# A two-block transformer kernel: pointwise work of the mixers done behind the tiles of the input projection, and the modulation sums of block two moved

## The reference, cut to what matters

```python
mod = cond @ ada_w[l] + ada_b[l]          # six vectors: sh1, sc1, g1, sh2, sc2, g2
h = _rms_norm(x, norm1_g[l]) * (1.0 + sc1) + sh1
pa, pb, pc, pd = _split(h @ w_in[l], GROUP_COLS)
# a, recurrent mixer
p = p + (p_prev - p) * mu                 # shift by one token, all of group a
w_log = -softplus(-(w0 + tanh(wd) @ w_up)) - 0.5
a = sigmoid(a0 + ad @ a_up)
g = sigmoid(gd) @ g_up                    # low-rank gates
# b, difference attention: q, k normed per 32 columns, rotated
# c, gating mixer
u, v = _split(gelu(p), C_SIZES)
v = _layer_norm(v, ln_g, ln_b)            # then mixed over tokens, times u
# d, forgetting attention: q, k normed per 64 columns
log_f = log_sigmoid(fl + f_b); F = cumsum(log_f)
x = x + g1 * (y @ w_out[l])
h = _rms_norm(x, norm2_g[l]) * (1.0 + sc2) + sh2
x = x + g2 * _conv_glu_ffn(h, ...)
```

## Time and profile before

| | us |
|---|---|
| runs | 2949.37, 2945.52, 4985.75 (median 2949.37) |
| the profiled execution, its own time | 2949.65 |
| its span, first to last instruction | 2947.9 |
| PE busy | 2452.9 (83%) |
| DVE busy | 1565.0 (53%) |
| ACT busy | 1107.3 (38%) |
| POOL busy | 397.8 (13%) |
| mean granted TensorE clock | 0.891 of full |

### The profile page before, as it was taken

One profiled execution on the slowest core, in us unless ns is written; L12 is line 12 of the kernel. 1 busy time (PEld: TensorE's weight loads), 2 busy tenths in 40 slices (PEclk: granted clock), 3 DMA queues, 4 the chain that ended last, 5 costly groups with the idle time before them and its releaser, 6 DMA issues. The chain is left out here.

```text
span 2947.9 us, 33176 instructions
## 1 busy us (share of the span) xinstructions
PE 2452.9 (83%) x11740; PEld 1944.6 (66%) x11740; DVE 1565.0 (53%) x2218; ACT 1107.3 (38%) x1651; POOL 397.8 (13%) x271
## 2 busy tenths in 40 slices
PE   2996788799989797878879998969977896598984
PEld 1884565578868586557558886847855675477773
DVE  4445656445555344465635555531137643578885
ACT  2224434333331222433433333132234423477773
POOL 0000110000000000010000000000004411566663
PEclk9996899899999798789889999979976687799997
DMA  6540000122234353000012223422115220799994
GB/s 260 193 141 1 1 29 1 57 93 98 94 109 149 104 206 112 1 1 29 8 65 93 92 85 119 145 72 72 57 50 204 64 83 30 294 357 358 363 361 161
DMA packets 94909, 354.73 MB, mean 120 GB/s; under 512 B 12736, under 2 KB 14416, under 8 KB 92496
## 3 DMA queue, kind: packets, MB, share of 16 engines
q1 hardware_dynamic: 87344, 329.16, 31.5%
q0 software_dynamic: 4288, 14.69, 1.5%
q10 hardware_dynamic: 3168, 9.45, 0.8%
HBM read 339.60 MB, written 22.04 MB: 123 GB/s over the span
## 5 line engine op out<-in xcount | busy, mean ns | idle before, releaser
L498 PE MATMUL ps<-a_hi,w_hi 128*128 128x512 f32 x1408 | 564.3, 401 | 80.0 <-PEq L351 58.0
L500 PE MATMUL ps<-a_hi,w_lo 128*128 128x512 f32 x1408 | 564.4, 401 | 0.0
L462 DVE TENSOR_TENSOR w_lo<-ring,w_hi 128x1024 fp32r<-128x1024 f32 x184 | 225.0, 1225 | 570.6 <-ACT w_hi L457 570.6
L499 PE MATMUL ps<-h_lo,w_hi 128*128 128x512 f32 x1280 | 504.4, 394 | 0.0
L457 ACT ACTIVATE w_hi<-ring 128x1024 fp32r<-128x1024 f32 x184 | 194.3, 1058 | 627.8 <-PE ps L500 613.7
L498 PEld LDWEIGHTS ps<-a_hi,w_hi 128*128 128x128 f32 x1408 | 268.6, 191 | 144.6 <-issue 61.5
L500 PEld LDWEIGHTS ps<-a_hi,w_lo 128*128 128x128 f32 x1408 | 267.9, 190 | 65.9
L499 PEld LDWEIGHTS ps<-h_lo,w_hi 128*128 128x128 f32 x1280 | 243.8, 190 | 60.0
L2654 DVE TENSOR_TENSOR moe_w_lo<-p,moe_w_hi 128x1024 fp32r<-128x1024 f32 x144 | 241.6, 1714 | 65.1 <-ACT moe_w_hi L2752 64.6
L2752 ACT ACTIVATE moe_w_hi<-p 128x1024 fp32r<-128x1024 f32 x216 | 228.6, 1062 | 98.4 <-PE ps L2695 97.4
L2654 POOL TENSOR_TENSOR moe_w_lo<-p,moe_w_hi 128x1024 fp32r<-128x1024 f32 x72 | 181.3, 2518 | 144.1 <-ACT moe_w_hi L2752 144.1
(11 more groups left out here) (564 smaller groups left out, 4679.6 us busy)
## 6 DMA issues: line engine op xcount, KB each, us to landing
ring<-in_ffn_up SPq DMA_DIRECT2D x88, 512.0 KB, 3.5
p<-in_moe_gate SPq DMA_DIRECT2D x72, 512.0 KB, 5.8
p<-in_moe_up SPq DMA_DIRECT2D x72, 512.0 KB, 7.5
p<-in_moe_down SPq DMA_DIRECT2D x72, 512.0 KB, 6.1
vt<-in_ada SPq DMA_DIRECT2D x64, 512.0 KB, 4.5
ring<-in_w_in SPq DMA_DIRECT2D x48, 512.0 KB, 3.6
ring<-in_ffn_down SPq DMA_DIRECT2D x16, 1408.0 KB, 6.5
p<-in_ada SPq DMA_DIRECT2D x32, 512.0 KB, 5.4
```

Of the source, the lines that this page charges most:

```text
L462: self.c.nc.vector.tensor_tensor(self.c.w_lo[:, s % 2, :], self.c.slot(s), self.c.w_hi[:, s % 2, :].bitcast(F32), ALU.subtract).then_inc(s ...
L498: nc.tensor.matmul(bank, c.w_hi[:, s % 2, at], hi(kt), start=(kt == 0), stop=False)
L499: nc.tensor.matmul(bank, c.w_hi[:, s % 2, at], lo(kt), start=False, stop=False)
L500: ins = nc.tensor.matmul(bank, c.w_lo[:, s % 2, at], hi(kt), start=False, stop=(kt == KT - 1))
```

## The change

Block one. The columns of `w_in` are reordered on the host so that group a comes first, then the forget gates, group c, group d and group b last. A new stage `project_in` takes the place of `split_stage` for the input projection. It is written out in full instead of as a loop, has two piece buffers for the modulation sums instead of four, and does behind the tiles: the shift, the low-rank inputs, decay and rate, the Gelus and the gating norm, the forget gates and their scan, and the norms of the forgetting attention's four query and key tiles. What stays in the mixers: the gate products of group a, the transpose and mixing of group c, and preparing steps for group b alone. The plan's formula is the same, and so the first part now spreads 2 + 8 attention steps over 30.

Block two. The modulation sums are added by DVE behind the 12 tiles of the second GLA projection, from two buffers, into the places of tables that are no longer needed. PE's 64 small matmuls and the bias follow the second preparing step of the first head. The transposed keys are kept in two copies, one for each half of the rows, with the other half zero, so that the state updates are products of 128 rows.

The new stage:

```diff
+def project_in(c, lin, sums):
...
+    share = lambda t: range(t * sums.pieces // lin.n, (t + 1) * sums.pieces // lin.n)
...
+    with nc.Block() as block:
+        @block.sync
+        def _(sp):
+            sp.dma_start(lora_w, c.dram["rw_lora"][bass.ds(c.layer, 1), :, :].rearrange("a p n -> p (a n)")
+                         ).then_inc(e["loaded"], 16)
+            sums.load_bias(sp, [c.mod[:, 2 * KT:]])
+            for t in range(lin.n):
+                for n in share(t):
+                    if n >= len(sums.piece):
+                        sums.load(sp, n)
+                if t + RING < lin.n:
+                    lin.load_one(sp, t % RING, t // RING + 1)
...
+        @block.tensor
+        def _(pe):
+            def early(t):
+                if t == 9:
+                    pe.wait_ge(e["loaded"], 16)
+                    pe.wait_ge(e["tanh"], 2)
+                    for q in range(2):
+                        for i, r in enumerate((slice(0, 32), slice(32, 64))):
+                            nc.tensor.matmul(bank(2 * q + i), lora_w[r, q * P:(q + 1) * P], lora[r, :], start=True, stop=True,
+                                             tile_position=(32 * i, 0)).then_inc(e["lora"], 1)
+                if t == 13:
+                    for i in range(2):
+                        pe.wait_ge(e["gelu"], 3 + i)
+                        last = nc.tensor.matmul(bank(0), c.const("ones"), gv[i], start=(i == 0), stop=(i == 1))
+                    last.then_inc(e["mean"], 1)
+                if t == 16:
+                    for i in range(2):
+                        pe.wait_ge(e["squared"], i + 1)
+                        last = nc.tensor.matmul(bank(1), c.const("ones"), g_sq[i], start=(i == 0), stop=(i == 1))
+                    last.then_inc(e["var"], 1)
+                k = t - 18
+                if 0 <= k < 4:
+                    pe.wait_ge(e["qk_sq"], k + 1)
+                    if k >= 2:
+                        pe.wait_ge(e["qk_ln"], k - 1)
+                    nc.tensor.matmul(bank(2 + k % 2), c.const("bo64"), sq[k % 2], start=True, stop=True).then_inc(e["qk_ss"], 1)
+
+            for t in range(lin.n):
+                if t >= RING:
+                    pe.wait_ge(lin.emptied, t - RING + 1)
+                pe.wait_ge(lin.low, t + 1)
+                lin.products(t, c.ps[:, t % RING, :], (lambda kt: c.a_hi[:, kt, :], lambda kt: c.h_lo[:, kt, :])
...
+                early(t)
...
+        @block.scalar
+        def _(act):
+            on = nc.scalar.activation
+
+            def early(t):
+                if t == 8:
...
+                    on(lora[0:32, :], m[0:32, :], ACT.Tanh).then_inc(e["tanh"], 1)
+                    on(lora[32:64, :], m[32:64, :], ACT.Copy).then_inc(e["tanh"], 1)
+                    on(lora[64:128, :], m[64:128, :], ACT.Sigmoid).then_inc(e["tanh"], 1)
+                if t == 10:
+                    for q in range(2):
+                        act.wait_ge(e["lora"], 2 * q + 1)
+                        on(decay[q], bank(2 * q), ACT.Sigmoid, bias=c.col("rw_w0", q)).then_inc(e["sig"], 1)
+                        act.wait_ge(e["lora"], 2 * q + 2)
+                        on(rate[q], bank(2 * q + 1), ACT.Sigmoid, bias=c.col("rw_a0", q)).then_inc(e["sig"], 1)
+                if t == 12:
+                    act.wait_ge(lin.emptied, T_C + 4)
+                    for x in (*gu, *gv):
+                        on(x, x, ACT.Gelu).then_inc(e["gelu"], 1)
...
+                if t == 13:
...
+                    on(gate, gate, ACT.Identity, bias=c.col("fx_f_b")).then_inc(e["f_in"], 1)
...
+                    on(f_abs, gate, ACT.Abs).then_inc(e["f_in"], 1)
+                if t == 14:
+                    act.wait_ge(e["f_in"], 2)
+                    on(f_abs, f_abs, ACT.Exp, scale=-1.0).then_inc(e["f_in"], 1)
+                    act.wait_ge(e["f_in"], 3)
+                    on(f_abs, f_abs, ACT.Ln, bias=1.0).then_inc(e["f_exp"], 1)
+                if t == 15:
+                    for i in range(2):
+                        act.wait_ge(e["centred"], i + 1)
+                        on(g_sq[i], gv[i], ACT.Square).then_inc(e["squared"], 1)
+                if t == 17:
+                    act.wait_ge(e["var"], 1)
+                    on(g_rs, bank(1), ACT.Ln, bias=c.const("eps"), scale=1.0 / 256).then_inc(e["rs"], 1)
+                    act.wait_ge(e["rs"], 1)
+                    on(g_rs, g_rs, ACT.Exp, scale=-0.5).then_inc(e["rs"], 1)
+                k = t - 17
+                if 0 <= k < 4:
+                    act.wait_ge(lin.emptied, T_D + k + 1)
+                    if k >= 2:
+                        act.wait_ge(e["qk_ss"], k - 1)
+                    on(sq[k % 2], qk[k], ACT.Square).then_inc(e["qk_sq"], 1)
+                k = t - 19
+                if 0 <= k < 4:
+                    act.wait_ge(e["qk_ss"], k + 1)
+                    if k == 0:
+                        act.wait_ge(e["f_neg"], 1)
+                    if k == 1:
+                        act.wait_ge(e["normed"], 4)
...
+                    on(rs[k % 2], bank(2 + k % 2), ACT.Ln, bias=c.const("eps"), scale=1.0 / 64).then_inc(e["qk_ln"], 1)
+                    act.wait_ge(e["qk_ln"], k + 1)
+                    on(rs[k % 2], rs[k % 2], ACT.Exp, scale=-0.5).then_inc(e["qk_rs"], 1)
...
+            for t in range(lin.n):
+                if t + 2 < lin.n:
+                    lin.split_high(act, (t + 2) % RING, (t + 2) // RING)
+                act.wait_ge(lin.multiplied, t + 1)
+                on(c.p[:, t, :], c.ps[:, t % RING, :], ACT.Copy).then_inc(lin.emptied, 1)
+                early(t)
...
+        @block.vector
+        def _(dve):
+            eng = nc.vector
+
+            def early(t):
+                j = t - 1
+                if 0 <= j < 7:
+                    x, d = c.p[:, T_A + j, :], diff[j % 2]
+                    dve.wait_ge(lin.emptied, T_A + j + 1)
...
+                    eng.tensor_tensor(d[:, 1:S], x[:, 0:S - 1], x[:, 1:S], ALU.subtract).then_inc(e["shifted"], 1)
+                    eng.tensor_scalar(d[:, 0:1], x[:, 0:1], -1.0, None, ALU.mult).then_inc(e["shifted"], 1)
...
+                    eng.scalar_tensor_tensor(x, d, c.col("rw_mu", j), x, ALU.mult, ALU.add).then_inc(e["shifted"], 1)
+                if t == 14:
+                    dve.wait_ge(e["mean"], 1)
+                    for i in range(2):
+                        eng.scalar_tensor_tensor(gv[i], bank(0), -1.0 / 256, gv[i], ALU.mult, ALU.add
+                                                 ).then_inc(e["centred"], 1)
+                if t == 15:
+                    dve.wait_ge(e["f_exp"], 1)
+                    eng.scalar_tensor_tensor(gate, gate, 0.0, f_abs, ALU.min, ALU.subtract).then_inc(e["f_in"], 1)
+                    dve.wait_ge(e["f_in"], 4)
+                    eng.tensor_tensor_scan(f_neg, c.const("ones", 1).to_broadcast([P, S]), gate, 0.0, ALU.mult, ALU.subtract
+                                           ).then_inc(e["f_neg"], 1)
+                    eng.tensor_scalar(q_gain, c.col("fx_q_g"), 64 ** -0.5, None, ALU.mult).then_inc(e["f_neg"], 1)
+                if t == 18:
+                    dve.wait_ge(e["rs"], 2)
...
+                    for i in range(2):
+                        eng.scalar_tensor_tensor(gv[i], gv[i], c.col("sg_ln_g", i), g_rs, ALU.mult, ALU.mult
+                                                 ).then_inc(e["normed"], 1)
...
+                        eng.tensor_scalar(gv[i], gv[i], c.col("sg_ln_b", i), None, ALU.add).then_inc(e["normed"], 1)
+                k = t - 20
+                if 0 <= k < 4:
+                    dve.wait_ge(e["qk_rs"], k + 1)
...
+                    eng.scalar_tensor_tensor(qk[k], qk[k], gain, rs[k % 2], ALU.mult, ALU.mult).then_inc(e["qk"], 1)
...
+            for t in range(lin.n):
+                if t + 2 < lin.n:
+                    lin.split_low(dve, (t + 2) % RING, (t + 2) // RING)
+                for n in share(t):
+                    sums.add(dve, n)
+                early(t)
```

What goes from the mixers, and what changes there:

```diff
-T_A, T_B, T_C, T_D = 0, 7, 13, 17
+T_A, T_B, T_C, T_D, T_F = 0, 18, 8, 12, 7
...
         finish_bias(eng)
-        yield
-
...
-    steps = dict(first=1, gating=4, prepare=PREP, forget=NU + 1, diff=NU + 2)
...
+    steps = dict(first=1, gating=2, prepare=PREP, forget=NU + 1, diff=NU + 2)
...
+            eng.matmul(PS(2 + q), lora_w[64:128, q * P:(q + 1) * P], lora[64:128, :], start=True, stop=True,
+                       tile_position=(64, 0)).then_inc(sh["lora"], 1)
...
+            eng.wait_ge(sh["lora"], q + 1)
+            on(keep[q]["gate"], PS(2 + q), ACT.Copy).then_inc(sh["gate"], 1)
         yield
...
-            eng.wait_ge(sh["dve"], 3 * i + 2)
-            eng.scalar_tensor_tensor(x, d, c.col("rw_mu", j), x, ALU.mult, ALU.add).then_inc(sh["dve"], 1)
-        eng.wait_ge(sh["dve"], 21)
...
+                            if g == 0 and q == 0:
+                                eng.wait_ge(att["biased"], 1)
```

(69 more changed lines are left out.)

271 lines of the change are left out of this document (83 added, 188 removed).

## The result

The changed kernel takes 2876.07 us (2872.76 to 2878.19), the kernel before 2949.93 in the same comparison: ratio 0.9753, 95% interval 0.9734 to 0.9773. That is 74 us less where I forecast 56. The run of 4985.75 us of the kernel before is left out of the ratio.

What follows compares the result with a forecast made beforehand. PE bounds both projections; waits set the time in the mixers' start and the heads. Plus 10.6 and minus 30.4 a layer, twice, is minus 39.6; with block two's minus 16.1, minus 55.7 from 2949.65: 2894, range 2862 to 2930.

Steps and rivals of the forecast that it cites:

- the padding: Heads of block two: padding the keys to 128 rows shortens nothing, as the update's columns stay 256, at 0.40 us each.
- (E): Slower: two piece buffers set the time of three stages; at a landing of 9 us about 3004; chance 0.07.
- (D): Second GLA projection: landings of 5 to 6 us cost 10 to 25 us more, 2905 to 2920; chance 0.1.
- the mixing at 9.7 us: Mixers: PE's mixing of group c takes 9.7 us, between 7.7 at a high clock and 11.9 at 0.60.
- my 30.4: Mixers: minus 30.4 us a layer, from 25.0 at L1529, 3.4 for four L804 and 2 of the rotation wait.
- The lower bound of 24: Mixers: the smallest gain, minus 24 us a layer, with mixing at 11.9 us and nothing from the rotation wait.
- Rival (C): Mixers: the new wait behind the mixing and POOL's copies take back 10 us a layer, 2914; chance 0.2.
- the low end of my bounds: Mixers: delay of DVE's chain by POOL's five copies, bounds 0 and 4.9 us a layer, taken as 0.
- tail for 7.3: Second GLA projection: behind the last copy come an addition, hand-over and landing, and an addition, plus 7.3 us; bounds 3 and 16.
- my terms (plus 9.5, minus 22): Heads of block two: plus 9.5 us for the 64 sums and bias, minus 22 for shorter scans and L2117.
- Rival (B): Closed gaps keep PE at 2.4 GHz in heads and mixers' starts: 23 us more gained, 2871; chance 0.18.
- The row that I held against it: Heads, 2256 to 2260 us: PE busy all 4.00 us yet clock 0.53, taken as evidence against closed gaps lifting the clock.

## Why the forecast was right, and where it was not

The direction held, and the mechanism in all steps but one, the padding, which I had at nothing. That the sum came as near as it did is in part luck: in two terms errors cancelled, named below.

**Input projection.** PE stayed the bound and everything else was covered. The first copy of a tile and the last one, after and before:

```profile
77.47 0.58 ACT L1614 ACTIVATE p<-ps 128x512 f32<-128x512 f32 x1
...
213.57 0.60 ACT L1614 ACTIVATE p<-ps 128x512 f32<-128x512 f32 x1 [3.72 <-PE ps L476]
```

```profile
78.66 0.58 ACT L576 ACTIVATE p<-ps 128x512 f32<-128x512 f32 x1
...
205.81 0.60 ACT L576 ACTIVATE p<-ps 128x512 f32<-128x512 f32 x1 [4.96 <-PE ps L500]
```

That is 136.1 us for 127.2: 9.0 for twelve products where I had 10.3. The four low-rank ones, of 32 rows each, cost about 2 together (1.99 from first to last) and not 3.4; the others cost 0.86 each, as taken from the earlier trace rows. The rest of the difference is a first tile that ended 1.3 us earlier. Two buffers sufficed; the median landing was 3.7 us. Rivals (E) and (D) did not occur. The load of the other engines came as added up, ACT 58.14 us for 59 and DVE 81.24 for 83.

**Mixers.** I had the mixing at 9.7 us and in the first layer it took 9.6. That was luck: I took the 7.7 us of the earlier trace rows for a mixing at a high clock and scaled them up to 11.9, but the clock over these 7.7 us was 0.66, and wherever it is 0.50 throughout, the mixing takes 9.7. In the second layer it took 7.5. The clamp came 2 us later than I placed it, and all behind it. At the second half's clamp 25.8 us are gained in the first layer, where my 30.4 were all to be had by then. That the stage still gained 31.0 and 33.4 us comes from behind it, 5 us in the first layer, which I had at nothing; what gave them I did not trace. The lower bound of 24 does not come out of its own conditions either, 30.4 less 2.2 and 2 being 26. Rival (C) named the right wait; moved away it is worth 7 us a layer, but the sum had it. POOL's copies did touch DVE's chain: L1390 took 0.98 us and L1392 1.99 for its two instructions; in the kernel with the mixing moved, where no copy stood beside them, 0.69 and 1.41. That is 0.9 us in the first layer's first half, near the low end of my bounds.

**Second GLA projection.** 5.3 of tail for 7.3. No row stood behind the 0.4 that I had for hand-over and issue; the trace shows both with the landing as 3.5 us, from the end of the first of the two additions (about 2119.1) to 2122.59, where I had 4.7. The median landing was 3.8 us. The remaining difference is that the stage had ended 1.0 us behind the copy before, and now ends 0.3 behind the last addition.

**Heads: the step that failed.** "Padding the keys to 128 rows shortens nothing." Without it the heads to the router are 23.5 us shorter than before, of which 10.6 are the output projection's; that leaves 12.9, and my terms (plus 9.5, minus 22) give 12.5. Here too errors cancelled: the first scans came 10.6 us later in their stage, not 9.5, and the scans before the change had taken 3.74, 7.67, 9.70 and 9.70 us in the four heads, not long in two and somewhat less in the last, which is 16 us all the same. With it they are 33.5 shorter. The padding is the 10 us of difference, the term that I had at nothing. I weighed it by the products' columns alone, and so did the rule that I cited from the Trainium skill, "TensorE: Matmul & The Clock Gate", "LDWEIGHTS (loading the stationary operand)": at an equal clock that holds here (a load for the updates takes 182 ns at the shortest and 335 at the longest with 64 rows, 186 and 337 with 128), but the clock was not equal. Rival (B) had the right place and size (15 of its 23 us were for the heads) and the wrong cause: with the gaps gone and 64 rows the clock stayed at 0.65. The row that I held against it, PE busy 4.00 of 4 us at 0.53, was the sign: a full PE at 1.2 GHz, with products of 64 rows in it (12 of its 20). The Trainium skill's sentence, same page, "What's actually happening", that the clock follows how busy PE has been, is not enough here: 40.45 of 44 us busy gave 0.66 and 34.19 of 41 gave 0.88.

## What to carry to other kernels

Where PE is busy and its granted clock stays low, look at the rows of its products, and test it by padding; in the heads an operand padded with zeros to 128 rows was worth 10 us, as much as removing a wait, but nothing where PE waited for DVE. Before you call a clock the effect of an edit, look at every pass through the same code in every profile you have: the mixing looked like a second proof until its second layer was read. When work is moved out of a stage, read the order anew: what is left moves closer together, and a step that stood in a gap (the mixing, the sums) may now stand in front of the chain. Ask of every bulk operation of POOL which DVE operations run beside it, the small ones too.

## What the runs showed of the hardware that I had not expected

- In the heads the granted clock of a stretch followed the rows of PE's products: 0.66 with 64 rows, 0.88 with 128, at the same work. In the mixing the same code with 4 rows ran at either clock, 2.07 or 1.2 us for the same eight products.
- Additions of POOL beside DVE stretched a scan set from 3.74 to 9.67 us and an operation of 24 elements from 0.18 to 2.27, and with 43 us of them in a head of 62, DVE's work of 27 us became 45. Only operations with their inputs in SBUF were stretched; one with an input in PSUM took 1.65 us for four beside POOL and 1.66 without.
- Products of 32 rows side by side at two places of the array cost PE some 0.5 us each (four in 1.99 us from 126.49 us on), where one of 128 rows costs 0.86.
